# Cached keys spread over the compressed chain, with identity products behind each later key unit: a decoder trunk on one Trainium2 core

## What is computed

```python
def nsa_cmp_sel(q, q_rot, qpos, kvc, kvs, pe_k, pe_v, w_ck, w_cv):
    ck = compress(kvc[:, :, 0], pe_k, w_ck)          # compressed keys, one per 32 positions
    cv = compress(kvc[:, :, 1], pe_v, w_cv)
    s = jnp.einsum('bqghd,bngd->bqghn', qg, ck) * SCALE
    p = masked_softmax(s, cmask[None, :, None, None, :])
    o_cmp = jnp.einsum('bqghn,bngd->bqghd', p.astype(cv.dtype), cv)
...
    o_sel = sel_attend(q_rot, qpos, idx, kb, vb)     # the best 16 blocks of 64 positions
def win_attend_cached(qr, qpos, kr, vr, kpos):
    s = jnp.einsum('bqghd,bkgd->bqghk', qg, kr) * SCALE
```

## Time and profile before

| | |
|---|---|
| median of 3 runs | 2461.63 us (2459.86 to 2465.2) |
| the profiled execution: its own time | 2456.92 us |
| its span in the trace | 2455.1 us |
| PE busy | 2393.0 us (97%) |
| DVE busy | 1560.7 us (64%) |
| ACT busy | 1069.2 us (44%) |

### The profile page before, as it was taken

One profiled execution on the slowest core, in us unless ns is written; L12 is line 12 of the kernel. 1 busy time (PEld: TensorE's weight loads), 2 busy tenths in 40 slices (PEclk: granted clock), 3 DMA queues, 4 the chain that ended last, 5 costly groups with the idle time before them and its releaser, 6 DMA issues. The chain is left out here.

```text
span 2455.1 us, 51122 instructions
## 1 busy us (share of the span) xinstructions
PE 2393.0 (97%) x20524; PEld 2265.4 (92%) x20524; DVE 1560.7 (64%) x2011; ACT 1069.2 (44%) x1263; POOL 94.1 (4%) x180
## 2 busy tenths in 40 slices
PE   7999998999999999999999999999999999999996
PEld 6788862779999999999999999999999999999996
DVE  6777688675775555465465778758745645545556
ACT  3333321454554353354354455435634534543543
POOL 0000013320000000000000100000000000000000
PEclk9999999999999999999999999999999999999998
DMA  9999569895546555555545564454555545454441
GB/s 385 345 326 322 206 221 326 302 337 200 195 174 214 198 208 202 205 205 198 187 172 188 176 220 166 149 183 172 177 183 175 184 175 186 171 186 174 179 181 70
DMA packets 102829, 516.79 MB, mean 210 GB/s; under 512 B 13072, under 2 KB 29520, under 8 KB 56496
## 3 DMA queue, kind: packets, MB, share of 16 engines
q1 hardware_dynamic: 91728, 467.90, 53.3%
q0 software_dynamic: 10976, 47.13, 5.5%
HBM read 508.59 MB, written 18.95 MB: 215 GB/s over the span
## 5 line engine op out<-in xcount | busy, mean ns | idle before, releaser
L1554 DVE TENSOR_TENSOR wlo<-wraw,whi 128x2048 fp32r<-128x2048 f32 x356 | 815.2, 2290 | 595.2 <-ACT whi L1080 594.8
L1080 ACT ACTIVATE whi<-wraw 128x2048 fp32r<-128x2048 f32 x356 | 682.0, 1916 | 1028.7 <-PE psa L438 1023.1
L436 PE MATMUL psa<-xhi,whi 128*128 128x266 f32 (+1 forms) x3632 | 1044.6, 288 | 17.5 <-DVE wlo L1554 15.7
L437 PE MATMUL psa<-xlo,whi 128*128 128x266 f32 (+1 forms) x3632 | 1039.8, 286 | 0.0
L438 PE MATMUL psa<-xhi,wlo 128*128 128x266 f32 (+1 forms) x3632 | 1038.7, 286 | 0.0
L436 PEld LDWEIGHTS psa<-xhi,whi 128*128 128x128 f32 x3632 | 688.0, 189 | 33.2 <-DVE wlo L1554 16.8
L437 PEld LDWEIGHTS psa<-xlo,whi 128*128 128x128 f32 x3632 | 688.7, 190 | 0.2
L438 PEld LDWEIGHTS psa<-xhi,wlo 128*128 128x128 f32 x3632 | 686.1, 189 | 0.0
L438 PE MATMUL psa<-hhi,wlo 128*128 128x264 f32 x2048 | 581.4, 284 | 0.0
L437 PE MATMUL psa<-hlo,whi 128*128 128x264 f32 x2048 | 581.3, 284 | 0.0
L436 PE MATMUL psa<-hhi,whi 128*128 128x264 f32 x2048 | 580.9, 284 | 0.0
(11 more groups left out here) (403 smaller groups left out, 1298.4 us busy)
## 6 DMA issues: line engine op xcount, KB each, us to landing
wraw<-in_w SPq DMA_DIRECT2D x356, 1024.0 KB, 4.8
page<-in_cmp SPq DMA_DIRECT2D x128, 384.0 KB, 5.5
kbuf<-in_selk SPq DMA_DIRECT2D x64, 192.0 KB, 4.2
kbuf<-in_selk POOLq DMA_DIRECT2D x64, 192.0 KB, 4.3
vbuf<-in_selv SPq DMA_DIRECT2D x64, 192.0 KB, 4.2
vbuf<-in_selv POOLq DMA_DIRECT2D x64, 192.0 KB, 4.2
o_win<-in_win POOLq DMA_DIRECT2D x8, 1533.0 KB, 8.2
kbuf<-in_wink SPq DMA_DIRECT2D x8, 768.0 KB, 5.4
```

Source lines behind the costliest of these rows:

```text
L436: mm(out, wh, hi[:, k, 0:w], start=(k == 0), stop=False)
L437: mm(out, wh, lo[:, k, 0:w], start=False, stop=False)
L1080: A(whi[:, p % 2, :], wraw[:, p, :], ACT.Copy).then_inc(s.hi_ready, 1)
L1554: V.tensor_tensor(wlo[:, p % 2, :], wraw[:, p, :], whi[:, p % 2, :].bitcast(F32), ALU.subtract).then_inc(s.lo_ready, 1)
```

## The change

Five key units lie earlier in PE's program, and small products are added behind the later ones. Units 3, 5 and 7 directly follow 2, 4 and 6, and all four groups g = 0 to 3 get a pair of units, so that 12 units instead of 8 lie ahead of the compressed sums. The r loop then has 12 instead of 16: two units at even r and one at odd r. Behind each key unit from r = 2 on, and in each of the eight rounds of the compressed output, `keep_busy(3)` multiplies the identity with itself three times (128 x 128 by 128 columns, float32) into the turning bank that comes next. Nobody reads that. `keep_busy(0)` has only the wait of `flip_bank()`.

```diff
-            keys(next(key_units))
-            keys(next(key_units))
+            def key_pair():
+
+                keys(next(key_units))
+                keys(next(key_units))
+
+            key_pair()
             pe.wait_ge(s.pk_prod, 1)
...
-            keys(next(key_units))
+            key_pair()
             pe.wait_ge(s.imp_read, 1)
             plain_queries(0)
-            keys(next(key_units))
...
             for g in range(KVH):
-                if g:
-                    keys(next(key_units))
+                key_pair()
                 if g < 3:
                     plain_queries(g + 1)
                 block_scores(g)
-            keys(next(key_units))
+
+            def keep_busy(n):
+
+                out = flip_bank()
+                for _ in range(n):
+                    mm(out[:, 0:128], ident, ident, start=True, stop=True)
...
                 keys(next(key_units))
-                keys(next(key_units))
+                if r % 2 == 0:
+                    keep_busy(3 if r > 1 else 0)
+                    keys(next(key_units))
+                keep_busy(3 if r > 1 else 0)
                 if r == 2:
                     turned_queries(0)
...
                     keys(next(key_units))
+                    keep_busy(3)
```

## The result

The changed kernel took 2467.83 us in the median of 11 runs (2463.8 to 2475.43), the kernel before 2461.63 (2455.37 to 2465.41, 11 runs beside it). The ratio is 1.0034, with a 95% interval of 1.0024 to 1.0044: slower by 8.4 us (5.9 to 10.8). The medians differ by 6.2. The forecast was 2466.6. The profiled execution took 2467.67 us, its span 2465.8.

A forecast was written before the change was run, and what follows sets the result against it. DVE's full list was taken to bound the attention before bank 2, PE the rounds once products were added. Later bank 2 (+0.67) and seven rounds (+4.27) gave +4.94 on 2461.63, so 2466.6 us; range 2461 to 2471.

The forecast's parts named there:

- turned queries start: PE begins turning the queries at 367.56 us, 4.41 later than 363.15, behind two more pairs and the products.
- DVE's wait for it: DVE waits 2.67 us at line 1833 for ACT's exponential, which ends at 371.11 behind the copies of the turned queries.
- one group of products: Three identity products on PE are six passes of 0.136 us, 0.82 us, priced from line 815.
- seven rounds: Second round to score loop: PE sets the pace, 22.65 us where before it took 18.38, so +4.27.
- The bound of the gain from earlier keys: PE's idle time before bank 2 mostly covers DVE's work; earlier keys can give at most DVE's 2.00 us wait.
- The cheap product: Rival: a product group costs 0.36 us, so the change adds only +0.8, 2462.4 us; chance 0.11.
- the rivals without the wait: Rival: turned queries come by 364.9, so no DVE wait at line 1833; +2.3, 2463.9 us; chance 0.10.
- with late keys: Rival: loads of units 20 to 23 land 4 us later, PE sets bank 2; +1 more, 2467.6 us; chance 0.06.
- The slow spell at 383: Sign: the slow key passes behind PE's 1.41 us wait for unit 21's keys would be gone.
- the clock falls once in the new gap: Rival: PE's clock drops while it waits for DVE before round two; +1.5, 2468.1 us; chance 0.13.
- The last condition named for being wrong: The forecast is wrong if score loop to end of span changes by more than 1 us.
- nothing is given back: From the score loop on, key units and values are unchanged and PE is full, so the loss stays whole.

The follow-up runs named there:

- The second experiment: The changed kernel with ACT's exponential of the compressed scores put ahead of its copies of the turned queries: 2461.85 us, ratio 1.0008 to the kernel before.
- the first experiment: The changed kernel without any identity product, so the new key order alone (waits of `keep_busy(0)` stay): 2459.15 us, ratio 0.9997 to the kernel before.
- the one with the exponential first: The changed kernel without products, ACT's exponential ahead of its copies, DVE's convolution steps left where they were: 2460.67 us, ratio 1.0003 to the kernel before.
- the experiment that filled the gap: The changed kernel with twelve instead of three identity products behind the first of the eight rounds: 2466.46 us, ratio 1.0026 to the kernel before.

## Why the prediction was nearly right, and where its reasoning was off

The changed kernel's first profile is read here less what the change doesn't touch: 1.55 of the early spell, less 0.53 of an earlier start, together 1.02. Its second profile has no early spell and starts 0.39 earlier than the kernel before, which is added. Up to the second round the two agree within 0.1 us, but for PE's arrival at the first, where nobody waits for it.

| step | forecast | first profile, less 1.02 | second, plus 0.39 |
|---|---|---|---|
| turned queries start | 367.56 | 367.41 | 367.41 |
| exponential ends | 371.11 | 370.92 | 370.91 |
| DVE's wait for it | 2.67 | 2.70 | 2.60 |
| PE at the first round | about 388 | 387.83 | 388.14 |
| DVE takes bank 2 | 391.41 | 391.29 | 391.28 |
| second round starts | 393.47 | 393.34 | 393.34 |
| one group of products | 0.82 | 0.86 | 0.87 |
| seven rounds | 22.65 | 22.88, and 3.10 of slow spell | 22.88, and 1.58 of slow spell |
| score loop | 416.1 | 419.3 | 417.8 |

**What held.** The chain was the one forecast: products and two more pairs push the turned queries back, ACT's strict list carries that to the exponential, DVE waits, and the keys that now come early are waited for by nobody. The two pairs moved ahead cost 5.87 us (32.30 for 26.43 up to the sums), where the forecast had 6.02; with that, bank 2 goes 0.54 later than before instead of 0.67. The second experiment shows that link by cutting it: +2.0 instead of +8.4. The order alone made a wait of 0.92, the change one of 2.70; the difference of 1.78 is two groups of products (1.72) ahead of the turned queries. The bound of the gain from earlier keys (2.00 us, all cover for DVE) held in the first experiment, where no gain was measured, and in the one with the exponential first. The price of a product was right within 5%. By the Trainium skill ("TensorE: Matmul & The Clock Gate", "Back-to-back issue gap") an estimate for six passes is 0.34 us with the 56 ns that the forecast took from it, which the section gives for the isolated product, and 0.49 with its 81 ns for a stream of weight loads and products; the trace has 0.86, 2.5 and 1.8 times as much. The cheap product is ruled out, and so are the rivals without the wait (it was 2.70 and 2.60) and with late keys (waits of 0.59 and 0.42 in the earlier trace rows's place, none before bank 2). The slow spell at 383 did vanish: with products behind the late key units all six profiles are without it, and of the eight without products seven have it. That can be worth no more than a part of the 2.00 us which DVE waited for keys.

**What was off.** The step that was wrong is the clock: the sum puts it at nothing and leaves it to the rival "the clock falls once in the new gap", with a chance of 0.13 and a price of 1.5 us. In both profiles of the changed kernel it is the case, at 3.10 and 1.58 us. The price came from a single odd unit; in the first profile the spell took in a whole round. The forecast had computed the gap itself, PE done at about 390.7 and round two at 393.47, 2.8 us, and the row beside it showed slow passes behind a wait of only 1.41. The argument against, that products keep PE busier ahead of it, is refuted: three of them stand directly ahead of the gap, at full clock. With the spell as the main case the forecast would have been 2468.1 to 2469.7. The range held the result all the same. That the median lies only 1.2 us above the forecast is in part luck: the ratio puts the loss at 8.4, 1.7 times the +4.94 of the sum. And the chances hardly leaned to slower, 0.48 against 0.47 for no difference.

**The size.** Up to the score loop the two profiles have +6.62 and +8.14: 0.54 for bank 2, 4.50 for the rounds, and a spell of 1.58 or 3.10. The ratio's +8.4 (5.9 to 10.8) and the medians' +6.2 both agree with that. The last condition named for being wrong did come true: from the score loop to the end the span differs by 1.5 us (2045.5 and 2043.9). The forecast of "nothing is given back" holds for the waits, which are the same; what differs is how long the clock is down at the same places, and this differs between two profiles of one kernel too (2044.4 in the second one of before, 2044.3 in the second one of the change). So the condition was set too tight for this kernel, and it does not speak against the mechanism.

**What is not settled.** Why the products alone cost as much as the whole change (+8.1), when the attention of their own trace is only 3 to 5 longer (224.0 us, where the kernel before has 219.1 and 221.3). Outside the attention the spans of the 14 profiles differ by as much as the change costs, 2235.3 to 2242.4 us, and 2247.7 in that one; no run shows what from. Open is also what share of the measured +8.4 is the spell, since the experiment that filled the gap can't be told from the change in time.

## What to carry to other kernels

Idle time on one engine is only worth its length less what the next engine in line covers: here PE's idle 4 us in ten hid DVE's full list, and at most 2.00 could be won. Work put in to keep an engine busy has a price per pass, and whoever puts it ahead of a hand-over must follow what the strict list behind that hand-over delays; a wait of 2 to 4 microseconds made there also cost the clock afterwards, in all five profiles that had one. And the ordering that brought nothing alone (0.9997), with the list's order repaired and DVE's surplus moved out, was part of a version 0.2% faster than the kernel before (0.9981, 0.9969 to 0.9992): count the two engines that take turns together, since neither's relief shows without the other's.

## What the runs showed of the hardware

- **The clock behind a gap in the rounds.** Of 14 profiles, five had PE idle for 1.99 us or more before the second round (1.99, 2.17, 2.42, 2.73, 3.83), and all five ran slow directly behind it; nine had 0.7 or less there, and none did. By the granted clock of single microseconds it fell while PE still waited in four of them (behind 2.42 us of idle time PE was at work again for half a microsecond). The length of the spell varies: about 7 us in one profile of the changed kernel and 3 in the other, with nearly the same gap, and nearly 14 in the profile of the key order alone, with the shortest gap of the five. The seven rounds were longer for it by 1.55 to 5.11 us. A wait of 2.46 at the end of the attention stands in all 14 profiles. In eleven it is followed by eight passes of line 847 (836 or 846 in other kernels) in 1.10 us, full speed, and in the first profile of the changed kernel the clock is at 0.50 less than two microseconds later; in three the passes were slow at once (1.55, 1.94 and 1.99).
- **A spell that belongs to no kernel.** Behind the 32 passes with four columns (line 750 before, 754 after), nine of the 14 profiles had slow key passes and five had not, each of the two kernels compared once with and once without. PE is never idle ahead of it. Up to the compressed sums it cost 1.6 us in four of the nine and 3.2 in the other five, and a comparison of two single profiles would put it down to the change. In the changed kernel DVE takes bank 2 later by as much (1.56 us between its two profiles, counted from the first key unit).
- **POOL's queue.** Two stores at unit 20, moved to unit 36, brought the first round 4.75 us forward (390.39 to 385.64), and the wait for unit 20's keys from 4.28 to 0.70. The two stores are 496 and 60 KB and took 7.9 and 6.9 us from issue to landing. What between the stores and the key issues takes that long was not measured by itself.
